# Gate columns beside the attention columns, tables and identity made elsewhere on GpSimd, and one group of twelve filling products per level of the inverse

## The reference

```python
h = silu(x @ w_gate) * (x @ w_up) @ w_down        # D_FF = 2816, twice in a layer
u = rms_norm(x) @ w_in                            # 1024 -> 3080
# A) 4 heads x 64, rotary, three dilation patterns merged by their denominators
# B) trailing means over 2, 4, 8, 16 positions, a 64x64 map for each group, a scale
# C) 4 heads x 128, causal conv on q, k, v, then per chunk of 64:
beta, g = sigmoid(b), -exp(a_log) * softplus(a + dt_bias)   # b, a: the last 8 columns of w_in
T = inverse(eye + A)                              # A strictly lower triangular
v_new = u_i - w_i @ state ;  o = (q_i * exp(g)) @ state + a_i @ v_new
o = rms_norm(o) * silu(z)
y = concat(A, B, C) @ w_out                       # 256 + 256 + 512 -> 1024
```

## Time and profile before

| | |
|---|---|
| time, median of 3 runs | 1051.43 us (1051.27 to 1051.48) |
| profiled execution | 1051.6 us, of which the span of its instructions is 1049.8 us |
| mean granted clock of PE | 0.998 of 2.4 GHz |
| PE busy | 1027.4 us, 98% of the span |
| DVE busy | 740.4 us, 71% |
| ACT busy | 606.0 us, 58% |
| POOL busy | 226.9 us, 22% |
| mixer of layer 0 / layer 1 (first attention product to last output product) | 141.98 / 140.75 us |

### The profile page before, as it was taken

The page is one execution under the profiler, slowest core; times in us unless marked ns, Lnnn a source line. Parts: engine busy times, 40 slices in busy tenths (PEclk is TensorE's granted clock), DMA queues, the critical chain, the costliest instruction groups (busy, mean ns, idle before and its releaser), DMA issues.

```text
span 1049.8 us, 19002 instructions
## 1 busy us (share of the span) xinstructions
PE 1027.4 (98%) x6488; PEld 888.7 (85%) x6488; DVE 740.4 (71%) x1197; ACT 606.0 (58%) x1066; POOL 226.9 (22%) x256
## 2 busy tenths in 40 slices
PE   6999999999999999999999999999999999999997
PEld 5888888899887888888888888889989778888885
DVE  5766666799776776666686666668986777666665
ACT  6655555777554655555575555557774465555554
POOL 2311111089400221111122111112013003111111
PEclk9999999999999999999999999999999999999999
DMA  8966666585123576666647666665831337666661
GB/s 260 260 187 194 181 192 187 142 225 158 54 69 101 152 210 193 191 192 185 197 124 220 192 186 186 196 175 136 230 101 62 90 92 221 201 192 186 187 193 40
DMA packets 252041, 176.92 MB, mean 169 GB/s; under 512 B 7939, under 2 KB 237592, under 8 KB 251864
## 3 DMA queue, kind: packets, MB, share of 16 engines
q1 hardware_dynamic: 250880, 174.41, 57.3%
q0 software_dynamic: 336, 1.36, 0.4%
q10 hardware_dynamic: 776, 0.49, 0.2%
HBM read 175.19 MB, written 1.05 MB: 168 GB/s over the span
## 4 chain that ended last, share of the span: by engine, by line
PE 86%; POOL 5%; DVE 3%; ACT 2%; issue 2%; DMA 0%; DVEq 0%; ACTq 0%; POOLq 0%
PE bank L700 28%; PE bank L703 15%; PE bank L682 12%; PE bank L683 11%; PE bank L684 11%; PE bank L709 1%; PE bank L1081 1%; PE bank L1068 1%; POOL qT L554 1%; DVE xr L2000 1%; DVE X L1826 1%; PE bank L1001 1%; POOL gact L594 1%; DVE Wl L1789 1%; ACT X L1410 1%
## 5 line engine op out<-in xcount | busy, mean ns | idle before, releaser
L1789 DVE TENSOR_TENSOR Wl<-raw,Wh 128x1024 fp32r<-128x1024 f32 x328 | 421.6, 1292 | 80.6 <-ACT Wh L1341 80.2
L1341 ACT ACTIVATE Wh<-raw 128x1024 fp32r<-128x1024 f32 x328 | 335.5, 1054 | 78.7 <-PE bank L684 77.9
L700 PE MATMUL bank<-X,Wh 128*128 128x512 f32 x1344 | 334.7, 391 | 0.1
L700 PEld LDWEIGHTS bank<-X,Wh 128*128 128x128 f32 x1344 | 246.7, 188 | 47.7 <-issue 0.2
L594 POOL TENSOR_TENSOR gact<-gact,pooled 128x256 f32<-128x256 f32 x88 | 78.6, 893 | 607.6 <-DVE gact L1878 462.2
L703 PEld LDWEIGHTS bank<-X,Wl 128*128 128x128 f32 x1344 | 183.1, 190 | 13.8 <-DVE Wl L1789 0.9
L703 PE MATMUL bank<-X,Wl 128*128 128x256 f32 x1344 | 187.7, 282 | 0.0
L682 PE MATMUL bank<-Wh,aH 128*128 128x512 f32 x336 | 132.4, 394 | 1.4 <-DVE aL L1899 1.4
L683 PE MATMUL bank<-Wl,aH 128*128 128x512 f32 x336 | 131.7, 392 | 0.0
L684 PE MATMUL bank<-Wh,aL 128*128 128x512 f32 x336 | 130.8, 389 | 0.0
L1447 ACT ACTIVATE dec<-bank 128x256 f32<-128x256 f32 x88 | 33.7, 383 | 123.4 <-PE bank L703 123.4
(11 more groups left out here) (277 smaller groups left out, 1262.3 us busy)
## 6 DMA issues: line engine op xcount, KB each, us to landing
raw<-in_ffn_w_gate SPq DMA_DIRECT2D x88, 512.0 KB, 4.0
raw<-in_ffn_w_up SPq DMA_DIRECT2D x88, 512.0 KB, 3.9
raw<-in_ffn_w_down SPq DMA_DIRECT2D x88, 512.0 KB, 4.4
raw<-in_w_in SPq DMA_DIRECT2D x48, 512.0 KB, 4.8
raw<-in_w_out SPq DMA_DIRECT2D x16, 512.0 KB, 3.4
cst<-in_consts POOLq DMA_DIRECT2D x1, 1188.0 KB, 5.8
xr<-in_x SPq DMA_DIRECT2D x2, 512.0 KB, 4.4
out_x<-big SPq DMA_DIRECT2D x3, 256.0 KB, 2.0
```

The lines of the kernel that those rows point to most:

```text
L700: nc.tensor.matmul(b[:, :], piece(Wh, s)[:, k, :], X[:, k, :, :], start=k == 0, stop=False)
L1341: return nc.scalar.activation(Wh[:, s, :], raw[:, s, :], ACT.Copy).then_inc(hi_cast.sem, 1)
L1789: return nc.vector.tensor_tensor(Wl[:, s, :], raw[:, s, :], Wh[:, s, :].bitcast(F32), ALU.subtract).then_inc(lo_cast.sem, 1)
```

## The change

It has six parts, and none changes what is computed.

1. The gate columns ride beside attention pieces 4 and 5: the slots of `Wh` and `Wl` have room for 132 columns in each block, and the two attention parts over these pieces stream 264 columns instead of 256. The gate weights of both layers (`gate_raw`) are loaded once, by two transfers that POOL issues; ACT casts their high part and DVE their low part in one small instruction each per layer. ACT copies the gate columns straight from the attention banks. The gate piece, its 8 products, the 4 turning products, the multiply and the copy on DVE go.
2. The tables are made on POOL in FFN 1 of layer 0, four steps after each tile from the second on. The low part of `X` moves from POOL to DVE. The first q piece takes its products with `Wl` last, and `row_root`, the product that spreads the row scale, moves into the third attention part.
3. The identity and the ones are made by POOL (two memsets and an `affine_select`) in place of a transfer. Before the turns PE runs four products of 256 columns, whose result nothing reads, and the quarters of `x` are turned in another order.
4. In the inverse P and D follow each other, and all twelve filling products stand behind D; so too in the quarter and the half step.
5. Behind the inverse the heads' attention weights have buffers of their own, the first is turned through bank 5, the pooled maps stand ahead of L1269's product, and the first piece of the output projection right behind the first turn of weights; DVE and ACT follow.
6. `first_pair` in its three later uses has the last turn between the two halves of its low products.

```diff
@@ gate columns: PE @@
+                width = WITH_GATES if pos in GATE_PIECES else P
-                    m = three(b, xh[:, k, t], xl[:, k, t], Wh[:, pair, k * P:(k + 1) * P],
-                              Wl[:, pair, k * P:(k + 1) * P], i == 0, i == KT - 1)
+                    w = slice(k * width, (k + 1) * width)
+                    m = three(b, xh[:, k, t], xl[:, k, t], Wh[:, pair, w], Wl[:, pair, w], i == 0, i == KT - 1)
...
-                for k in range(KT):
-                    m = nc.tensor.matmul(bank[1][0:2 * GATES, :], gate_weights[:, k, :, :], X0[:, k, :, :],
-                                         start=k == 0, stop=k == KT - 1)
-                m.then_inc(gates_proj.sem, 1)
@@ POOL: identity, tables, transfers @@
+            made(nc.gpsimd.memset(ident, 0.0))
+            made(nc.gpsimd.memset(ones, 1.0))
+            pool.wait_ge(ident_made.sem, 2)
+            made(nc.gpsimd.affine_select(out=ident.unsqueeze(1), in_=ident.unsqueeze(1), compare_op=ALU.not_equal, fill=one,
+                                         base=0, pattern=[[0, 1], [-1, P]], channel_multiplier=1))
...
+                    def next_tile(step):
+
+                        if step % TRIG_STEPS == 0:
+                            scale_tile(layer, tile[0], tile[0] % 2)
+                            tile[0] += 1
+
+                    for _ in range(2):
+                        next_tile(0)
+                    trig_tables(next_tile)
...
-            pool.dma_start(cst[:, C_FIRST:], consts[:, C_FIRST:]).then_inc(masks_in.sem, 16)
+            for l in range(DEPTH):
+                pool.dma_start(gate_raw[:, l, :, :], cols(w_in, l, IN_WIDTH - GATES, GATES)).then_inc(gate_raw_in.sem, 16)
+            pool.dma_start(cst[:, C_FIRST:], consts[:, :]).then_inc(masks_in.sem, 16)
...
-                for p in range(KT // 2):
-                    b = slice(2 * p, 2 * p + 2)
-                    pool.wait_ge(*xs_hi.at(layer, p + 1))
-                    nc.gpsimd.tensor_tensor(Xl[:, b, :], xs[:, b, :], Xh[:, b, :].bitcast(F32),
-                                            ALU.subtract).then_inc(xs_lo.sem, 1)
-                if layer == 0:
-                    trig_tables()
@@ PE: head and first_pair @@
-                    pe.wait_ge(consts_in.sem, 16)
-                    for c, b in TURN_ORDER:
+                    pe.wait_ge(ident_made.sem, 3)
+                    for _ in range(WARM):
+                        nc.tensor.matmul(bank[7][:, 0:2 * P], ident, cst[:, C_IDENT:C_FIRST], start=True, stop=True)
+                    for c, b in ROW_ORDER:
...
-                    low(gbank[0], 0, left)
+                    low(gbank[0], 0, range(2))
                     between()
+                    low(gbank[0], 0, range(2, 4))
@@ PE: the inverse @@
-                    for c in range(HALVES):
-                        level_p(n, c)
-                    fill(range(k, k + 2))
-                    for c in range(HALVES):
-                        level_d(n, c)
-                    fill(range(k + 2, k + 4))
...
+                    for stage in (level_p, level_d):
+                        for c in range(HALVES):
+                            stage(n, c)
+                    fill(range(k, k + 4))
@@ PE: behind the inverse @@
+                turn_weights(0)
+                out_product(0)
+                turn_weights(1)
+                att_values(0)
+                out_product(1)
+                turn_weights(2)
+                att_values(1)
+                turn_weights(3)
+                att_values(2)
+                turn_out(0)
+                att_values(3)
+                turn_out(1)
+                out_product(2)
```

More of the change, by code:

```diff
@@ L107 @@
 Z_LEVELS = 2
+TRIG_STEPS = 4
+WARM = 4
 N_LEVELS = len(LEVELS) + 2
@@ L925, in mixer, with first_piece @@
                 enter_mixer(layer)
+                def first_piece():
+                    s, out = MIX_SLOTS[POS_QK], bank[0][:, 0:SEQ]
+                    pe.wait_ge(*hi_cast.at(layer, MIX_BASE + POS_QK + 1))
+                    for p in range(KT // 2):
+                        pe.wait_ge(*xs_lo.at(layer, p + 1))
+                        for k in (2 * p, 2 * p + 1):
+                            nc.tensor.matmul(out, piece(Wh, s)[:, k, :], Xh[:, k, :], start=k == 0, stop=False)
+                            nc.tensor.matmul(out, piece(Wh, s)[:, k, :], Xl[:, k, :], start=False, stop=False)
+                    split(POS_QK)
+                    for k in range(KT):
+                        m = nc.tensor.matmul(out, piece(Wl, s)[:, k, :], Xh[:, k, :], start=False, stop=k == KT - 1)
+                    return m
                 for i in range(8):
-                    split(POS_QK + i)
+                    if i < 3:
+                        pe.wait_ge(*att_read.at(layer, ATT_EARLY - 2 + i))
                     if i == 0:
-                        pe.wait_ge(*att_read.at(layer, ATT_EARLY))
-                    if i == 1:
-                        pe.wait_ge(*gates_copied.at(layer, 1))
-                    column_piece(bank[i][:, 0:SEQ], MIX_SLOTS[POS_QK + i],
-                                 (lambda p: pe.wait_ge(*xs_lo.at(layer, p + 1))) if i == 0 else None).then_inc(proj.sem, 1)
+                        first_piece().then_inc(proj.sem, 1)
+                    else:
+                        split(POS_QK + i)
+                        column_piece(bank[i][:, 0:SEQ], MIX_SLOTS[POS_QK + i]).then_inc(proj.sem, 1)
                 for h in range(2):
@@ L1264, in mixer @@
                 pe.wait_ge(*pool_copied.at(layer, 2))
-                pe.wait_ge(*vn_done.at(layer, 2))
-                pe.wait_ge(*qs_done.at(layer, 1))
-                for h in range(DN_HEADS):
-                    m = nc.tensor.matmul(bank[6][:, h * P:(h + 1) * P], aT[:, 4 + h, :], Vn[:, 4 + h, :], start=True, stop=True)
-                m.then_inc(o_ps.sem, 1)
-                turn_weights(0)
                 for j in range(2):
@@ L1416, in enter @@
                     act.wait_ge(zeroed.sem, 2)
-                    act.wait_ge(*turned.at(layer, 2))
+                    act.wait_ge(*turned.at(layer, 3))
                     for j in range(4):
@@ L1578, in mixer @@
                 hi_mix(layer, 5)
+                if layer == 0:
+                    act.wait_ge(gate_raw_in.sem, 16 * DEPTH)
+                nc.scalar.activation(with_gates(Wh)[:, :, :, P:], gates_of[:, layer, :, :, :], ACT.Copy).then_inc(gate_hi.sem, 1)
                 copy_half(2)
```

325 lines of the change are left out of this document (163 added, 162 removed).

## The result

The changed kernel takes 1042.88 us in the median of four executions (1040.92 to 1043.55), the one before 1051.45: a ratio of 0.9916, with a 95% interval of 0.9904 to 0.9928. The forecast was 1044.3, and the direction is the one forecast. The four executions lie 2.6 us apart, where those of before lie within 0.23.

The account below looks back on a forecast made before the run. PE, at 86% of the chain, was taken to bound the kernel. Against 1051.6 us, five PE terms gain 11.6 and the start gives 4.5 back, −7.1: 1044.5, or 1044.3 by the median; range 1038.5 to 1048.5.

Parts of the forecast that it names:

- no load at the select: Rival at the start: POOL's select loads nothing, the head gives −1.35 us in place of +3.2, whole 1039.8; chance 0.25.
- the prediction's own last sign: Prediction is wrong if the head moves by other than 3.2 us, or attention parts or first q piece wait for DVE.
- Gate columns: Both mixers: gate piece and turning products go from PE, −2.65 us a layer, −5.3 us in all.
- the 384 columns: Mixer: eight more columns in 48 products, priced at 0.16 us a layer at 2.4 GHz.
- Tables: Layer 0 mixer: PE's wait ahead of L983, where `grow` stands behind the tables on POOL, goes: −1.1 us.
- The inverse: Twelve fills in one group shorten a level from 3.91 to about 3.76 us; −1.2 us over two layers.
- The wait for the mask: Inverse: D must wait for DVE's mask, starting 1.06 us after P instead of 0.94; 0.12 us a level.
- Behind the inverse: Pooled maps fill the wait at L1269 (1.1 us), L1183's wait goes (0.74); −1.7 us a layer, −3.4 in all.
- `first_pair`: FFN starts: half the low products behind the last turn bring it 0.24 us sooner in three uses; −0.6 us.
- The head: Start: POOL's select pays a first-operation load, so splits begin at about 12.2 us in place of 8.97; +3.2 us.
- The gate weights' transfers: First FFN: two POOL issues of 1.0 us each ahead of the first scaling; +1.3 us (+0.5 to +12.3).
- The slow rival: Gate weight issues take time in proportion to runs, 6.5 us each, whole 1055.3 us; chance 0.07.

Follow-up runs that it names:

- e4: The kernel before with the high and low weight slots 1056 columns apart instead of 1024; 1054.58 us against 1051.41.
- e7: The changed kernel with the sine and cosine tables in the mixer of layer 0 again; 1044.59 us in one execution.
- e6: The changed kernel with the pooled maps behind the second product of the delta rule again; 1046.23 us in one execution.
- e8: The changed kernel with the last turn behind all four low products in the three later uses, as before; 1043.97 us in one execution.
- e3: The changed kernel with POOL issuing the two gate weight transfers after the second tile of the first FFN, not ahead of the first; 1041.41 us.
- e9: The kernel before with slots still 1024 columns apart, but 1536 bytes left free behind them; 1051.60 us.
- e10: The kernel before with the slots 1088 columns (4352 bytes) apart; 1051.62 us beside 1051.65 for the kernel before.
- e5: The changed kernel with the inverse's filling products in groups of six again, behind P and behind D; 1045.26 us in one execution.
- e2: The changed kernel with five more unread products of 256 columns between the last turn and the first product with weights; 1043.77 us.
- e1: The changed kernel without the four products of 256 columns ahead of the turns; 1042.37 us.
- e11: The changed kernel without the four products ahead of the turns and with the gate weights' transfers after the second tile; 1041.74 us.
- e12: The changed kernel without the four early products, with gate weight transfers after the second tile and slots 1088 columns apart instead of 1056; 1038.57 us.

## Why the prediction was right, and where it was not

The time came out within the range, 1.4 us under the predicted 1044.3, and faster as forecast. That it is so near is luck: the head was 5.7 us better than forecast, the tiles 3.1 worse, and the median execution is 2.0 worse than the profiled one. The mechanism at the start was the rival's, "no load at the select", to which the prediction gave a chance of 0.25 and a time of 1039.8. By the prediction's own last sign, a head that moves by another amount than 3.2 us, it was wrong there.

- *Gate columns*, forecast −5.3: measured −5.8 (2.9 in each layer). The mechanism was right: the gate piece and the turning products are gone from PE's list and nothing waits in their place. The 0.25 us a layer over the forecast isn't split up further, and no run puts the gate piece back by itself: that these 5.8 us are the gate columns' rests on the rows that are gone, and on layer 1, which has no tables and gained 2.9 alone.
- *Gate columns, the cost not seen.* The step that failed is the one that priced the wider slots with the 384 columns alone. The slots' distance touches every product with weights, and cost 3.1 us in the FFNs, over half of what the gate columns bring (e4: 3.2 us by itself).
- *Tables*, forecast −1.1: the amount is nearly right, the step isn't. It said that the tables' place holds `grow`; in e7 they stand in the mixer again, and that wait is gone. The tables there end 28 us sooner than before, of which 24 are their earlier start and the rest their shorter run; the start alone is enough to end a wait of 1.0 us. The tables' place is worth 0.9 us all the same, through DVE's longer casts and the waits behind them.
- *The inverse*, forecast −1.2: measured −1.8. The mis-sized term is the level: four levels take 14.86 us for 15.67 (first P of the first to the quarter step), 0.20 less each where the forecast had 0.15, which is 0.4 over two layers; the quarter step gave 0.0 for +0.05, and the half −0.09 for −0.05. The wait for the mask was sized right: D starts 1.05 us after P, for the 1.06 of the forecast, and 0.06 us after the mask is done (276.07). The rows can't tell it from P's own time, since 1.05 us is also what D takes to the first fill (278.84 − 277.79).
- *Behind the inverse*, forecast −3.4: measured −3.1. Both waits are gone as forecast, but the shares weren't as forecast: e6 shows the pooled maps to be worth 1.8 us a layer for the 1.1 forecast, since they also save the first output piece a wait, and the rest of the new order, forecast at −0.6 a layer, isn't seen as a gain without them (32.07 us in e6, 31.83 before).
- *`first_pair`*, forecast −0.6: about −0.5 by e8.
- *The head*, forecast +3.2: the step that failed is "I judge the select nearer to L554's case". The select took 0.29 us, behind its setting at 1.1 us. Of the three kinds of operation that stand behind such a setting in these two traces, one paid. The Trainium skill gives about 6 us for the first call to a kernel that has just been loaded (GPSIMD Engine Reference, § 2.1 Instruction dispatch); the 5.23 us of L554 are near it, and the select's 0.29 us show no such load. The rival without load, chance 0.25, had −1.35 at the first split; measured are −2.2 (6.77 for 8.97). In this trace the clock was up by 4.86, when the turns began, where 4.5 us after PE's first product would be 6.1; in the six other traces with these products the first split lies at 6.97 to 8.20, so that −0.8 to −2.2 were to be had.
- *The gate weights' transfers*, forecast +1.3: two issues took 1.87 us, 0.94 and 0.99 us each, for the 1.0 that I took. They cost 1.04 us (e3). The count of runs matters little: 1024 runs took 0.94 to 0.99 us where at most 128 took 0.59 to 0.81. The slow rival falls. By the Trainium skill, DMA: Bandwidth & Descriptors, § Anatomy of one DMA — SWDGE (gpsimd) path, many descriptors can be made before the increment shows; these rows agree in that the increment is 0.1 to 0.4 us for eight times the runs.
- *What was left out*: that the clock's rise differs from execution to execution, and that it can fall again. The changed kernel's executions differ by 2.6 us; the traces of its relatives show up to 1.4 us as a later rise and 1.6 us as a stretch of 3.4 us at the low level. Which of the two each of its other three executions had isn't shown.

## What to carry to other kernels

A buffer's new shape is paid by everyone who reads it: when a layout gets wider for one user, look at the distance of single products in the stages that the change doesn't touch, and try a second padding. A price that can be one of two far apart (here a load at the first operation) is worth more care than the terms that agree; a single case of each kind doesn't decide it. When a term turns out near its forecast, see whether the rows moved where it said: here one run put back part of the order and cost more than the forecast for it. Where a kernel's start makes its executions differ, one trace shows the lucky case: compare medians, and look for the low clock in several traces.

## What the runs showed of the hardware that was not expected

- Slots 4224 bytes apart in each partition made each of the 88 FFN tiles 0.036 to 0.041 us longer with no wait to be seen; 4096 and 4352 bytes did not (e4, e9, e10: 1054.58, 1051.60 and 1051.62 us).
- With PE's first product at 1.58 in seven traces, the clock's rise came before the first eight turns in two (1.04 us for the eight: the changed kernel and e3), during them in three (1.39 to 1.50 us: e5, e7, e8) and behind them in two (1.91 us: e2, e6).
- A fall to the low level of some 3.4 us, with products of 512 columns 0.43 us apart, stands in six of the ten traces of the changed kernel and its edits, at 10.6 to 11.4 us or at 26 to 28 us. All six have the four products at the start and the transfers ahead of the first scaling; the three without the products (e1, e11, e12), e3, and the four traces of the kernel before and its edits have none. One trace each doesn't show that either part makes it (e3's other three executions have a mean granted clock of 0.994, under that of any with a fall in its trace), and why it comes isn't settled.
- With the tables in the mixer (e7) PE has no wait for POOL there, and the mixer is still 0.9 us longer: beside POOL's table steps DVE's casts of 1024 columns took 1.438 us in the mean, for 1.214 without them (e1), while ACT's stayed at 1.055 us.
- With a select and its setting first on POOL (ten traces), no operation on POOL took over 2.3 us and the select 0.29, where the first of L554 takes 5.23 in all four traces without.
